# The pooling mixer's group products of a decoder layer on one core: three of four groups as split float32r operands in three passes, the splits made on ScalarE and GpSimd

## The reference, cut to what matters

```python
for g, w in enumerate(POOL_WINDOWS):          # windows 2, 4, 8, 16; one group of 128 channels each
    start = cs[:, s0:s0 + t_len, lo:hi]       # cs: running sum of u over the tokens
    cnt = jnp.minimum(pos + 1, w)
    means.append((end[..., lo:hi] - start) / cnt)
pooled = jnp.concatenate(means, axis=-1) - full[:, POOL_BUF:]
mixed = jnp.einsum('btgc,gcd->btgd', pooled.reshape(bsz, t_len, POOL_GROUPS, POOL_GC), w_pool)
mixed = mixed * pool_scale
...
mix = jnp.concatenate([y_pool, y_ml], axis=-1) @ w_out
x1 = _layer_norm(ALPHA * x + mix, ln1_g, ln1_b)
```

## Time and profile before

| | us |
|---|---|
| median of three runs | 1048.4 |
| lowest and highest | 1048.13, 1048.55 |
| the profiled execution, its own time | 1048.17 |
| its span in the trace | 1046.6 |
| PE busy | 1036.3 (99%) |
| VectorE busy | 747.9 (71%) |
| ScalarE busy | 495.6 (47%) |
| GpSimd busy | 101.6 (10%) |

### The profile page before, as it was taken

One profiled execution on the slowest core, in us unless ns is written; L12 is line 12 of the kernel. 1 busy time (PEld: TensorE's weight loads), 2 busy tenths in 40 slices (PEclk: granted clock), 3 DMA queues, 4 the chain that ended last, 5 costly groups with the idle time before them and its releaser, 6 DMA issues. The chain is left out here.

```text
span 1046.6 us, 19119 instructions
## 1 busy us (share of the span) xinstructions
PE 1036.3 (99%) x7761; PEld 1023.6 (98%) x7761; DVE 747.9 (71%) x1034; ACT 495.6 (47%) x711; POOL 101.6 (10%) x140
## 2 busy tenths in 40 slices
PE   9999999999999999999999999999999999999997
PEld 9999999999899999999999999999999999999986
DVE  6795775535797596876766767768766677887977
ACT  6554534345533576664664564565443323334223
POOL 3112221020211000000000000000000000000027
PEclk9999999999999999999999999999999999999999
DMA  9546996165224215245455445499634415325304
GB/s 283 144 176 153 246 199 135 61 165 126 71 102 141 102 41 216 98 142 185 129 157 185 141 153 183 148 296 344 229 122 166 159 62 182 122 93 172 122 3 160
DMA packets 97780, 159.95 MB, mean 153 GB/s; under 512 B 6485, under 2 KB 52277, under 8 KB 96681
## 3 DMA queue, kind: packets, MB, share of 16 engines
q1 hardware_dynamic: 88290, 127.72, 37.9%
q0 software_dynamic: 9152, 30.79, 11.3%
q10 hardware_dynamic: 270, 0.49, 0.2%
HBM read 111.56 MB, written 53.29 MB: 158 GB/s over the span
## 5 line engine op out<-in xcount | busy, mean ns | idle before, releaser
L2623 PE MATMUL bank<-x_hi,w_hi 128*128 128x344 f32 (+1 forms) x696 | 227.5, 327 | 0.2 <-DVE x_lo L1774 0.2
L2623 PE MATMUL bank<-x_hi,d_lo 128*128 128x258 f32 x968 | 222.4, 282 | 0.0
L2623 PE MATMUL bank<-x_lo,w_hi 128*128 128x344 f32 (+1 forms) x696 | 222.0, 319 | 0.0
L2623 PE MATMUL bank<-x_hi,w_lo 128*128 128x344 f32 x528 | 168.7, 319 | 0.0
L2623 PEld LDWEIGHTS bank<-x_hi,d_lo 128*128 128x128 f32 x968 | 165.7, 189 | 0.0
L2623 PEld LDWEIGHTS bank<-x_hi,w_hi 128*128 128x128 f32 (+1 forms) x696 | 130.4, 187 | 1.0 <-DVE x_lo L1774 0.5
L2623 PEld LDWEIGHTS bank<-x_lo,w_hi 128*128 128x128 f32 (+1 forms) x696 | 130.2, 187 | 0.4
L2623 PE MATMUL bank<-x_hi,s_hi 128*128 128x258 f32 x352 | 99.5, 283 | 0.0
L2623 PE MATMUL bank<-x_lo,s_hi 128*128 128x258 f32 x352 | 99.3, 282 | 0.0
L2623 PEld LDWEIGHTS bank<-x_hi,w_lo 128*128 128x128 f32 x528 | 99.2, 188 | 0.0
L2623 PE MATMUL bank<-t_hi,s_hi 128*128 128x258 f32 x336 | 95.2, 283 | 0.0
(11 more groups left out here) (463 smaller groups left out, 2570.7 us busy)
## 6 DMA issues: line engine op xcount, KB each, us to landing
h_ops<-h_unit SPq DMA_DIRECT2D x56, 258.0 KB, 7.3
x_lo_raw<-h_ops SPq DMA_DIRECT2D x14, 1032.0 KB, 5.3
s_raw<-in_w_ff SPq DMA_DIRECT2D x14, 1024.0 KB, 6.9
x_lo_raw<-h_ops SPq DMA_DIRECT2D x14, 774.0 KB, 4.5
d_raw<-in_w_ff SPq DMA_DIRECT2D x9, 1024.0 KB, 7.9
w_raw<-in_w_in SPq DMA_DIRECT2D x16, 512.0 KB, 7.1
h_ops<-t_out SPq DMA_DIRECT2D x28, 258.0 KB, 7.6
d_raw<-in_w_ff SPq DMA_DIRECT2D x8, 768.0 KB, 6.4
```

The source lines that it names most:

```text
L2623: return nc.tensor.matmul(out, lhsT, rhs, start=start, stop=stop, skip_group_check=True)
```

## The change

Groups 3, 2 and 1 of the mixer get split operands. ScalarE makes `w_pool_hi` (three groups of weights, 384 columns) and, for each of the three groups, `pooled_hi` (1032 columns) in float32r. GpSimd makes `w_pool_lo` (384 columns) and the lo part of each group's `pooled` (1032 columns), this one in place in `Y` (named `y_place` there), by `tensor_tensor` with both inputs in SBUF. PE then makes three float32r passes for each block of these groups instead of one float32 product. Group 0 stays as it was. On VectorE, `cat_lo_part(0, True)` goes behind the sums of group 0, and one wait on `mixed` is added ahead of the first product with the sample states, since `pooled_hi` lies where that product is written.

```diff
+            def pooled_lo(g):
+                pool.wait_ge(pool_hi, 5 - g)
+                G.tensor_tensor(YR[:, g, :], Y[:, g, :], PH[:, 3 - g, :].bitcast(F32), ALU.subtract).then_inc(pool_lo, 1)
...
                     elif h == NH - 1 and j == PAIRS - 1:
+                        pool.wait_ge(pool_hi, 1)
+                        G.tensor_tensor(WPL[:, 1:4, :], WP[:, 1:4, :], WPH[:, :, :].bitcast(F32), ALU.subtract).then_inc(pool_lo, 1)
+                        pooled_lo(3)
+                        pooled_lo(2)
                         pool.wait_ge(sn_out, 16)
                         pool.wait_ge(P_ready, NPAIR)
                         for q in range(4):
                             pool.dma_start(QKS[32 * q:32 * (q + 1), :, :],
                                            sn_d[0:2, :, 32 * q:32 * (q + 1)].rearrange("c r x -> r c x")).then_inc(qk_in, 16)
+                        pooled_lo(1)
...
+            def pool_w_hi():
+                act.wait_ge(small_in, 16 * 8)
+                act.wait_ge(qi_ready, NPAIR - 2)
+                A(WPH[:, :, :], WP[:, 1:4, :], ACT.Copy).then_inc(pool_hi, 1)
+
+            def pooled_hi(g):
+                act.wait_ge(pooled, 4 - g)
+                if g == 3:
+                    act.wait_ge(qi_ready, NPAIR)
+                    act.wait_ge(smp_kept, 3 * NH)
+                A(PH[:, 3 - g, :], Y[:, g, :], ACT.Copy).then_inc(pool_hi, 1)
...
+                    if (u, i) == (10, 5):
+                        pooled_hi(1)
...
+                    if (u, i) == (10, 3):
+                        pool_w_hi()
+                        pooled_hi(3)
+                        pooled_hi(2)
...
                 elif (u, i) == (10, 5):
-                    cat_lo_part(0, True)
                     window_first(0, n + 6)
                     window_last(0)
+                    cat_lo_part(0, True)
...
+                if x == 0:
+                    dve.wait_ge(mixed, 3 * 3)
...
             for i, g in enumerate((3, 2, 1, 0)):
-                pe.wait_ge(pooled, i + 1)
+                if g:
+                    pe.wait_ge(pool_lo, i + 2)
+                else:
+                    pe.wait_ge(pooled, 4)
...
-                    mm(bank[b][:, 0:BLK], WP[:, g, :], Y[:, g, blk(b)]).then_inc(mixed, 1)
+                    o = bank[b][:, 0:BLK]
+                    if g:
+                        mm(o, WPH[:, g - 1, :], PH[:, 3 - g, blk(b)], True, False)
+                        mm(o, WPH[:, g - 1, :], YR[:, g, blk(b)], False, False)
+                        mm(o, WPL[:, g, :], PH[:, 3 - g, blk(b)], False, True).then_inc(mixed, 1)
+                    else:
+                        mm(o, WP[:, g, :], Y[:, g, blk(b)]).then_inc(mixed, 1)
```

More of the change, by code:

```diff
@@ L196, in build_layer @@
         RSTD = at("r_std", [P, BLK], R["square_sum"])
+        PH = at("pooled_hi", [P, 3, NT], R["qkv1"] - 3 * XROW, F32R)
+        WPH = at("w_pool_hi", [P, 3, P], R["rows_bc"] - 8192, F32R)
+        WPL = at("w_pool_lo", [P, 4, P], R["w_pool_sb"] - 4 * 4 * P, F32R)
         WR = [at(f"w_out_rows{x}", [P, D], o_r1 + (6 + x) * XROW) for x in range(2)]
@@ L265, in build_layer @@
         pooled, mixed, mixed_read = sem("pooled"), sem("mixed"), sem("mixed_read")
+        pool_hi, pool_lo = sem("pool_hi"), sem("pool_lo")
         nat_T, nat_read, nat_out, outs = sem("nat_T"), sem("nat_read"), sem("nat_out"), sem("outs")
```

## The result

| | before | after |
|---|---|---|
| median of 10 runs each, same chip | 1048.22 us (1048.01 to 1048.63) | 1051.06 us (1050.43 to 1052.38) |
| ratio, 95% interval | | 1.0027 (1.0018 to 1.0035) |
| profiled execution | 1048.17 us, span 1046.6 | 1050.91 us, span 1049.3 |

The change makes the kernel 2.8 us slower. The forecast was 1051.1.

What follows compares the result with a forecast made beforehand. PE, busy 99% of the span, was taken as the bound; GpSimd's holds on VectorE would delay the output projection 2.9 us despite PE's 0.95 saving: 1048.17 + 2.9 = 1051.1 us, range 1047.3 to 1052.6.

Steps and rivals of the forecast that it cites:

- The hold: GpSimd's SBUF-reading subtractions and VectorE's two-SBUF-input operations block each other for a whole instruction, 2.4 us per 1032 columns.
- the upper bound: Cost to VectorE of one 2.4 us GpSimd operation: taken as the whole 2.4 us; lower bound 0.25.
- The walk on VectorE: VectorE's sums for group 1: 1023-column sum from 274.85, 1024-column sum 2.95 us late, group 1 finished at 281.4.
- The stand of PE: PE ahead of the `h_nat` transposes: ends group 3 at 280.6 and stands until 283.15.
- Group 0: Last mixing group: VectorE waits for GpSimd's group 1 until 285.9, finishes group 0 at 287.7, when PE starts it.
- The clock: PE's float32r steps in mixing and output projection: counted at 0.157 us each, with no fall of the clock forecast.
- the sum of 2.9: Output projection starts at 289.45 where it was in step at 286.54: 2.9 us late, carried to the end.
- the forecast's own range: Whole kernel, if the forecast's hold is right: 1050.2 to 1051.9 us, chance 0.52.
- PE's saving: Nine mixing products on PE, each 0.106 us shorter as three float32r passes: 0.95 us less in all.
- The rival of no hold: GpSimd's subtractions do not stop VectorE, group 1 stays at 278.47, PE wins 0.95 us: 1047.2 us; chance 0.19.
- ScalarE's copies: ScalarE's `pooled_hi` copies, 1.05 us each: hidden undisturbed; with the hold, group 1's runs 281.45 to 282.5 and delays `h_nat`.
- Nothing for the rest: After the mixing: the wait on `mixed` and later state reads cost nothing; PE and VectorE stay shifted by the delay.

Runs made afterwards that it cites:

- experiment 1: Changed kernel with GpSimd's subtractions cut to 8 columns (weights: 2 per group), lo parts left out of the result; 1047.59 us, ratio 0.9990.
- experiment 3: Changed kernel with PE mixing in float32 again, ScalarE's copies kept, GpSimd subtracting two different tiles into a scratch copy; 1052.43 us, ratio 1.0035.
- Experiment 4: Changed kernel with PE mixing in float32 again and GpSimd's subtractions replaced by memsets of about the same length; 1048.38 us, ratio 0.9994.
- experiment 5: Changed kernel plus 13 float32r products into a scratch bank where PE would stand ahead of the `h_nat` transposes; 1050.50 us, ratio 1.0020.
- experiment 9: Changed kernel with GpSimd's group 2 subtraction waiting for VectorE's 1023-column sum; 1051.53 us, ratio 1.0026, runs in two clumps: 1050.38 to 1050.73, 1051.10 to 1051.74.
- experiment 11: Changed kernel with GpSimd's group 2 waiting for VectorE's 1023-column sum and 13 extra float32r products on PE; 1051.28 us, ratio 1.0022.
- experiment 10: Changed kernel with only group 3 split, GpSimd's one long subtraction waiting for VectorE's 1023-column sum; 1048.16 us, ratio 0.9996.
- experiment 6: Changed kernel with ScalarE's copy of group 1 moved behind `h_nat`; 1051.98 us, ratio 1.0032.
- experiment 7: Kernel before the change, with only `cat_lo_part(0, True)` moved behind group 0's sums on VectorE; 1048.56 us, ratio 0.9999.
- experiment 2: Changed kernel with PE mixing in float32 again, ScalarE's copies kept, GpSimd subtracting each copy from itself in place; 1049.45 us, ratio 1.0006.

## Why the prediction was right

*The hold.* Right, in kind and size: VectorE's instruction stands until GpSimd's subtraction ends, and experiments 1 and 3 show it from both sides (gone without the length, there with PE's products left as they were). Experiment 4 shows that it takes GpSimd's reads. The Trainium skill's rule (SBUF — State Buffer, Who interferes with whom) that such a pair blocks each other whole, and that a GpSimd instruction which only writes SBUF does not, agrees with both: 2.68 us beside the subtraction, 1.22 beside the memsets. The evidence ahead of the run was 0.25 and 1.54 us; the choice of the upper bound, because the hold grew with the first instruction's length, was the step that decided. It rested on two rows, one for each direction, and none of them long on GpSimd's side.

*The walk on VectorE.* 0.4 us too late: group 1 at 281.4, measured 280.98. I had the 1023-column sum caught by the weights and group 3, and in fact the 8-column sum ahead of it was (2.38 us). The 1023-column sum began at 274.60, forecast 274.85. The small instructions ahead of a sum can be the ones that are held, and they cost as much.

*The stand of PE.* Forecast 280.6 to 283.15, measured a 2.0 us wait and the transposes at 282.64: the same 0.4 and 0.1 more. Right otherwise.

*Group 0.* Forecast 287.7, measured 286.69. GpSimd's subtraction of group 1 ended at 285.1 and not at 285.9, since all ahead of it was 0.4 earlier and its own wait 0.5 us (2.93 less 2.41) and not 0.95; and the instruction that was held, the one-column product, was already counted in what followed. 1.0 us too long.

*The clock.* Missed. I had all of PE's steps at 0.157 us; nine and more went at 0.287. So PE came to group 0 at 287.57, 8.70 us after the last attention matmuls, and not when `pooled` had come; with the clock up it was 286.98, 7.88 after them (experiment 5). In this execution the price was about 0.8 us, since the waits for GpSimd and for group 0 hid the rest; the clumps of experiment 9 lie 1.1 us apart. The two misses, group 0 a full 1.0 us too late and the clock forgotten, nearly cancel: PE's start of group 0 was forecast at 287.7 and measured at 287.57. That the sum of 2.9 meets the measured 2.74 (2.89 in the stretch) is luck in this part; with `pooled` forecast rightly and the clock left out it would have been 1.0 us lower, 1050.1, just below the 1050.2 at which I let the forecast's own range begin. The Trainium skill (TensorE: Matmul & The Clock Gate, What's actually happening) has the clock judged at moments that do not begin with the kernel, so that they fall otherwise from run to run. The mean clocks of the two clumps of experiment 9 agree with that; no run here tests it, and experiment 11 has high runs without the low clock.

*PE's saving.* Of the 0.95 us only 0.66 could reach the end even without the hold (experiment 1), since the division on VectorE, `h_nat` and ScalarE's first copy set the start of group 2. The working took each product as worth its 0.106 us wherever it stood. Three of nine products thus save nothing (experiment 10). The rival of no hold would have come near 1047.5 (1048.17 - 0.66; experiment 1 has 1047.59) and not at 1047.2.

*ScalarE's copies.* Right: two of 1032 columns took 2.01 us, and the one of group 1 pushed `h_nat` as forecast. Taking it away from there did not help (experiment 6), in which other things moved too.

*Nothing for the rest.* Right: the order of the sums costs nothing that the runs can show (experiment 7), and the delay is carried whole to the end.

## What to carry to other kernels

Count an elementwise operation given to GpSimd with its inputs in SBUF as time of VectorE's two-input operations on SBUF as well, unless VectorE then reads PSUM or idles; where VectorE does the same in half the time, as here, try it there. Read a hold as a long row and not as idle time: an 8-column sum of 2.38 us is the sign. And when a faster product stands behind a chain of three other engines, work out first when that chain lets it start: what PE saves ahead of that point it spends waiting.

## What the runs showed of the hardware

- TensorE's granted clock was 0.50 for about 3 us after a stand of 2.0 us. It fell also after a stand of 1.6 us (experiment 3, again about 3 us) and behind one of 1.7 us that a second of 1.0 followed (experiment 6, about 7 us). It was 1.00 after one of 2.2 us (experiment 9) and after one of 0.6 (experiment 2). With 13 extra products in the gap it was 1.00 in both profiled executions (experiments 5 and 11), and in experiment 5 PE was 0.75 us sooner at the projection.
- A GpSimd subtraction of 1032 columns took 2.41 us with two tiles as inputs and, by experiment 2, less with one tile as both: 1.90 us, and for 384 columns 0.83 against 1.02.
- Two memsets of 1032 columns took 1.98 us; two-input sums beside them kept 1.22 us, but a copy of 3 columns took 0.52 where 0.17.
- Who has the read when both engines ask at once differs between executions that are alike up to there: VectorE at 274.60 in the changed kernel, GpSimd at about 274.98 in experiment 6.
